# The softmax of a pair of heads, in operations common to both heads

## What is computed

```python
for i in range(S // Q_BLOCK):                 # two blocks of 128 queries
    s0, e = i * Q_BLOCK, (i + 1) * Q_BLOCK
    sc = (jnp.einsum('bqhd,bkhd->bhqk', q_nope[:, s0:e], k_nope[:, :e])
          + jnp.einsum('bqhr,bkr->bhqk', q_pe[:, s0:e], k_pe[:, :e]))
    sc = sc.astype(jnp.float32) * ATTN_SCALE
    mask = jnp.arange(e)[None, :] <= (s0 + jnp.arange(Q_BLOCK))[:, None]
    sc = jnp.where(mask, sc, -jnp.inf)
    p = jax.nn.softmax(sc, axis=-1).astype(v.dtype)
    outs.append(jnp.einsum('bhqk,bkhd->bqhd', p, v[:, :e]))
```

## Time and profile before

| | us |
|---|---|
| median of 3 runs | 1775.51 |
| lowest, highest | 1775.25, 1775.96 |
| the profiled execution | 1775.12 |
| its span, first to last instruction | 1773.2 |
| PE busy | 1762.1 (99%) |
| DVE busy | 1133.2 (64%) |
| ACT busy | 914.8 (52%) |
| POOL busy | 112.7 (6%) |

### The profile page before, as it was taken

One profiled execution on the slowest core, in us unless ns is written; L12 is line 12 of the kernel. 1 busy time (PEld: TensorE's weight loads), 2 busy tenths in 40 slices (PEclk: granted clock), 3 DMA queues, 4 the chain that ended last, 5 costly groups with the idle time before them and its releaser, 6 DMA issues.

```text
span 1773.2 us, 29180 instructions
## 1 busy us (share of the span) xinstructions
PE 1762.1 (99%) x10370; PEld 1560.7 (88%) x10370; DVE 1133.2 (64%) x1456; ACT 914.8 (52%) x1174; POOL 112.7 (6%) x132
## 2 busy tenths in 40 slices
PE   9999999999999999999999999999999999999998
PEld 5888888888888888889999888888888888888886
DVE  5766666556666666678997776666655566666553
ACT  6666664334444453456775456666533344445433
POOL 2200000000000001123111420000000000000000
PEclk9999999999999999999999999999999999999999
DMA  7555557545555566544445555555655455556642
GB/s 274 198 189 189 189 193 233 185 160 178 189 188 189 189 223 196 175 154 147 158 136 167 190 189 189 189 189 189 226 201 167 165 189 189 189 189 222 227 144 72
DMA packets 85728, 328.78 MB, mean 185 GB/s; under 512 B 9648, under 2 KB 10800, under 8 KB 85552
## 3 DMA queue, kind: packets, MB, share of 16 engines
q1 hardware_dynamic: 85536, 327.09, 55.1%
q10 hardware_dynamic: 144, 1.05, 0.2%
HBM read 326.01 MB, written 2.10 MB: 185 GB/s over the span
## 4 chain that ended last, share of the span: by engine, by line
PE 97%; DVE 2%; ACT 1%; issue 0%; POOL 0%; ACTq 0%; DVEq 0%; POOLq 0%
PE ps L427 57%; PE ps L428 31%; PE ps L497 1%; PE ps L435 1%; PE ps L437 1%; PE ps L436 1%; PE ps L787 1%; PE ps L786 1%; PE ps L788 1%; DVE w_lo L1210 0%; PE ps L623 0%; PE ps L625 0%; PE ps L624 0%; DVE xg L1220 0%; PE ps L677 0%; DVE x L1272 0%
## 5 line engine op out<-in xcount | busy, mean ns | idle before, releaser
L1210 DVE TENSOR_TENSOR w_lo<-raw,w_hi 128x1024 fp32r<-128x1024 f32 (+2 forms) x564 | 736.7, 1309 | 420.6 <-ACT w_hi L831 418.7
L427 PE MATMUL ps<-xg,w_hi 128*128 128x512 f32 x2880 | 999.7, 390 | 0.2 <-DVE w_lo L1210 0.2
L831 ACT ACTIVATE w_hi<-raw 128x1024 fp32r<-128x1024 f32 (+2 forms) x565 | 631.9, 1120 | 552.9 <-PE ps L428 537.1
L428 PE MATMUL ps<-xg,w_lo 128*128 128x256 f32 x2880 | 812.1, 282 | 0.0
L427 PEld LDWEIGHTS ps<-xg,w_hi 128*128 128x128 f32 x2880 | 540.7, 188 | 113.8 <-DVE w_lo L1210 0.6
L428 PEld LDWEIGHTS ps<-xg,w_lo 128*128 128x128 f32 x2880 | 544.3, 189 | 0.1
L427 PE MATMUL ps<-act,w_hi 128*128 128x512 f32 x1320 | 458.0, 390 | 0.0
L428 PE MATMUL ps<-act,w_lo 128*128 128x256 f32 x1320 | 372.2, 282 | 0.0
L427 PEld LDWEIGHTS ps<-act,w_hi 128*128 128x128 f32 x1320 | 247.8, 188 | 51.9
L428 PEld LDWEIGHTS ps<-act,w_lo 128*128 128x128 f32 x1320 | 249.5, 189 | 0.0
L1290 DVE TENSOR_TENSOR sums<-ps,cross 128x512 f32<-128x512 f32 x88 | 60.9, 692 | 95.5 <-ACT cross L908 95.2
(11 more groups left out here) (196 smaller groups left out, 1217.4 us busy)
## 6 DMA issues: line engine op xcount, KB each, us to landing
raw<-w_gate SPq DMA_DIRECT2D x176, 512.0 KB, 3.2
raw<-w_up SPq DMA_DIRECT2D x176, 512.0 KB, 3.2
raw<-w_down SPq DMA_DIRECT2D x120, 704.0 KB, 4.2
raw<-w_o SPq DMA_DIRECT2D x32, 512.0 KB, 3.2
raw<-w_last SPq DMA_DIRECT2D x11, 512.0 KB, 3.2
raw<-w_q_a SPq DMA_DIRECT2D x8, 512.0 KB, 3.2
raw<-w_kv_a SPq DMA_DIRECT2D x8, 512.0 KB, 3.2
raw<-w_q_nope SPq DMA_DIRECT2D x8, 512.0 KB, 3.7
```

Source lines behind the costliest of these rows:

```text
L427: pe.matmul(ps[:, bank, :], w_hi[:, s, j * P:(j + 1) * P], moving, start=start, stop=False)
L428: return pe.matmul(ps[:, bank, 0:SEQ], w_lo[:, s, j * P:(j + 1) * P], moving[:, 0:SEQ], start=False, stop=stop)
L831: nc.scalar.activation(dst, src, ACT.Copy).then_inc(hi_ready, 1)
L1210: nc.vector.tensor_tensor(lo, src, hi.bitcast(F32), ALU.subtract).then_inc(lo_ready, 1)
```

## The change

`row_max` and `normalise` now treat both heads of a pair in one call. `row_max` waits until the scores of both heads are there. The mask addition of the first block is one instruction for both heads, with the mask read twice through a broadcast. The two reductions of the second block follow, then one negation for both heads, then the cosine product (`rope_cos`, which stood between the heads), the two reductions of the first block and one negation. ACT waits once for the second block of both heads and does their two exponentials, then once for the first block of both and does theirs. `normalise` waits for all four, takes one reciprocal of four values a partition in place of two of two values each, and scales in four instructions as before. The targets of the waits change with the count; a pass of the loop has 12 counted steps on DVE in place of 16.

```diff
-            def exps(g, hh, i):
-
-                sc.wait_ge(max_ready, plus(4 * g + 2 * hh + 1, i, 8))
-                nc.scalar.activation(prob[:, hh, P:], prob[:, hh, P:], ACT.Exp, bias=stat[:, hh, 3:4],
-                                     accum_out=stat[:, hh, 5:6]).then_inc(exp_ready, 1)
-                sc.wait_ge(max_ready, plus(4 * g + 2 * hh + 2, i, 8))
-                nc.scalar.activation(prob[:, hh, 0:P], prob[:, hh, 0:P], ACT.Exp, bias=stat[:, hh, 2:3],
-                                     accum_out=stat[:, hh, 4:5]).then_inc(exp_ready, 1)
+            def exps(g, i):
+
+                sc.wait_ge(max_ready, plus(2 * g + 1, i, 4))
+                for hh in range(2):
+                    nc.scalar.activation(prob[:, hh, P:], prob[:, hh, P:], ACT.Exp, bias=stat[:, hh, 3:4],
+                                         accum_out=stat[:, hh, 5:6]).then_inc(exp_ready, 1)
+                sc.wait_ge(max_ready, plus(2 * g + 2, i, 4))
...
@@ -1486,28 +1486,35 @@
                                         heads[:, plus(g, i, 2), :, 0:SEQ].bitcast(F32),
                                         ALU.subtract).then_inc(head_split, 1)
 
-            def row_max(g, hh, i):
-
-                ve.wait_ge(scores_ready, plus(2 * g + hh + 1, i, 4))
-
-                scored, first, second = ps[:, SCORES + hh, :], prob[:, hh, 0:P], prob[:, hh, P:]
-                begun(nc.vector.tensor_tensor(first, scored[:, 3 * P:], const[:, C_MASK + P:C_MASK + 2 * P], ALU.add))
-                begun(nc.vector.tensor_tensor_reduce(second, scored[:, P:3 * P], const[:, C_MASK:C_MASK + 2 * P],
-                                                     ATTN_SCALE, -3.0e38, ALU.add, ALU.max, stat[:, hh, 1:2]))
+            def row_max(g, i, beside=lambda: None):
+
+                ve.wait_ge(scores_ready, plus(2 * g + 2, i, 4))
+                scored, both = ps[:, SCORES:SCORES + 2, :], prob[:, :, 0:P]
+                mask = const[:, C_MASK + P:C_MASK + 2 * P].rearrange("p (o t) -> p o t", o=1).broadcast_to([P, 2, P])
+                begun(nc.vector.tensor_tensor(both, scored[:, :, 3 * P:], mask, ALU.add))
+                for hh in range(2):
+                    begun(nc.vector.tensor_tensor_reduce(
+                        prob[:, hh, P:], scored[:, hh, P:3 * P], const[:, C_MASK:C_MASK + 2 * P], ATTN_SCALE, -3.0e38,
+                        ALU.add, ALU.max, stat[:, hh, 1:2]))
                 settled()
-                nc.vector.tensor_scalar(stat[:, hh, 3:4], stat[:, hh, 1:2], -1.0, None, ALU.mult).then_inc(max_ready, 1)
-                step(nc.vector.tensor_tensor_reduce(first, scored[:, 0:P], first, ATTN_SCALE, -3.0e38, ALU.add,
-                                                    ALU.max, stat[:, hh, 0:1]))
-                nc.vector.tensor_scalar(stat[:, hh, 2:3], stat[:, hh, 0:1], -1.0, None, ALU.mult).then_inc(max_ready, 1)
-
-            def normalise(g, hh, i):
-
-                ve.wait_ge(exp_ready, plus(4 * g + 2 * hh + 2, i, 8))
-                step(nc.vector.reciprocal(stat[:, hh, 6:8], stat[:, hh, 4:6]))
-                nc.vector.tensor_scalar(prob[:, hh, 0:P], prob[:, hh, 0:P], stat[:, hh, 6:7], None,
-                                        ALU.mult).then_inc(prob_ready, 1)
-                nc.vector.tensor_scalar(prob[:, hh, P:], prob[:, hh, P:], stat[:, hh, 7:8], None,
-                                        ALU.mult).then_inc(prob_ready, 1)
+                nc.vector.tensor_scalar(stat[:, :, 3:4], stat[:, :, 1:2], -1.0, None, ALU.mult).then_inc(max_ready, 1)
+                beside()
+                for hh in range(2):
+                    begun(nc.vector.tensor_tensor_reduce(
+                        prob[:, hh, 0:P], scored[:, hh, 0:P], prob[:, hh, 0:P], ATTN_SCALE, -3.0e38, ALU.add, ALU.max,
+                        stat[:, hh, 0:1]))
+                settled()
+                nc.vector.tensor_scalar(stat[:, :, 2:3], stat[:, :, 0:1], -1.0, None, ALU.mult).then_inc(max_ready, 1)
+
+            def normalise(g, i):
+
+                ve.wait_ge(exp_ready, plus(4 * g + 4, i, 8))
+                step(nc.vector.reciprocal(stat[:, :, 6:8], stat[:, :, 4:6]))
+                for hh in range(2):
+                    nc.vector.tensor_scalar(prob[:, hh, 0:P], prob[:, hh, 0:P], stat[:, hh, 6:7], None,
+                                            ALU.mult).then_inc(prob_ready, 1)
+                    nc.vector.tensor_scalar(prob[:, hh, P:], prob[:, hh, P:], stat[:, hh, 7:8], None,
+                                            ALU.mult).then_inc(prob_ready, 1)
 
             lat_norm(KV, 1, G_LKV, beside=(key_scale, lambda: None))
 
...
@@ -1526,11 +1533,8 @@
                 else:
                     if g >= 2:
                         heads_lo_half(g - 2, i)
-                    row_max(g - 1, 0, i)
-                    rope_cos(g, i)
-                    row_max(g - 1, 1, i)
-                    normalise(g - 1, 0, i)
-                    normalise(g - 1, 1, i)
+                    row_max(g - 1, i, beside=lambda: rope_cos(g, i))
+                    normalise(g - 1, i)
                     pair_lo(g, 1, q_buf, i)
                     split(n + SPLIT_SLOTS, i)
                     split(n + 1 + SPLIT_SLOTS, i)
@@ -1543,7 +1547,7 @@
 
             slot(0)
             slot(1)
-            loop(HG // 2 - 2, 2 * 8, lambda i: (slot(2, i), slot(3, i)))
+            loop(HG // 2 - 2, 2 * 6, lambda i: (slot(2, i), slot(3, i)))
             slot(HG - 2)
             slot(HG - 1)
 
```

More of the change, by code:

```diff
@@ L1051, in heads_hi_half @@
                                      ACT.Copy).then_inc(head_hi, 1)
-            def exps(g, hh, i):
-                sc.wait_ge(max_ready, plus(4 * g + 2 * hh + 1, i, 8))
-                nc.scalar.activation(prob[:, hh, P:], prob[:, hh, P:], ACT.Exp, bias=stat[:, hh, 3:4],
-                                     accum_out=stat[:, hh, 5:6]).then_inc(exp_ready, 1)
-                sc.wait_ge(max_ready, plus(4 * g + 2 * hh + 2, i, 8))
-                nc.scalar.activation(prob[:, hh, 0:P], prob[:, hh, 0:P], ACT.Exp, bias=stat[:, hh, 2:3],
-                                     accum_out=stat[:, hh, 4:5]).then_inc(exp_ready, 1)
+            def exps(g, i):
[5 more added lines that the diff above has]
+                for hh in range(2):
+                    nc.scalar.activation(prob[:, hh, 0:P], prob[:, hh, 0:P], ACT.Exp, bias=stat[:, hh, 2:3],
+                                         accum_out=stat[:, hh, 4:5]).then_inc(exp_ready, 1)
             def slot(g, i=None):
@@ L1082, in slot @@
                     split(n + SPLIT_SLOTS, i)
-                    exps(g - 1, 0, i)
-                    exps(g - 1, 1, i)
+                    exps(g - 1, i)
                     pair_hi(g, 1, q_buf, i)
@@ L1111, in _ @@
             split(n1 + SPLIT_SLOTS)
-            exps(HG - 1, 0, None)
-            exps(HG - 1, 1, None)
+            exps(HG - 1, None)
             split(n1 + 1 + SPLIT_SLOTS)
@@ L1553, in _ @@
             split(n1 + SPLIT_SLOTS)
[L1554 to L1557, removed]
+            row_max(HG - 1, None)
+            normalise(HG - 1, None)
             split(n1 + 1 + SPLIT_SLOTS)
```

## The result

The changed kernel takes 1780.64 us (median of 8 runs, 1780.15 to 1781.23) against 1775.30 for the kernel before (8 runs): 1.0031 of its time, 95% interval 1.0022 to 1.0041. It is slower, by 5.3 us where 5.1 was forecast (1780.6). One execution of neg_single, a kernel among the experiments, took 2171.76 us at a granted clock of 0.752 of full speed and is left out of its median.

A forecast was written before the change was run, and what follows sets the result against it. PE was taken as the bound, stalled by late L1480. Slots 2 to 6 cost 3.35 us, slot 1 0.37, slot 7 1.01, total 4.73; with 0.35 for issue, +5.1 on 1775.51 gives 1780.6 us, range 1777.0 to 1783.2.

The forecast's parts named there:

- (a): DVE's wait for both heads' scores: first mask moves by 0.94 us, to 0.32 behind the last score product's start.
- (b): From first mask addition to reciprocal, through reductions, negations and ACT's four exponentials: reciprocal starts 3.37 us after the mask.
- the open read: Accumulator's read behind the first of two reductions, shown by no row: taken as 0.05 us, bounds 0 and 0.12.
- (c): Normalisation, up to L1453: one reciprocal of 0.20 us and four scalings of 0.94 together, none overlapping POOL.
- (d): Instruction savings already counted; in the output projection's slot, later scaling put at nothing, or 0.6 us without cover.
- the issue gaps: Idle time at the cosine product in slot 2, now before the second negation: 0.35 us for both loop passes.
- the bounds that were given: Path from the first mask, for reads, semaphores and POOL: -0.16 to +0.36 us in each of seven slots.
- The first rival: Not slower: DVE's shorter work decides, not ACT's chain; mask to L1453 under 3.91 us, 1774.7 us; chance 0.12.
- The second: Rival: PE's stall comes but is under half, starts 0.3 us earlier; 2.6 us lost, 1778.1; chance 0.16.
- third: Rival: more is lost, issue gaps in both loop passes and POOL's collision in each slot; 6.9 us, 1782.4 up; chance 0.12.

The follow-up runs named there:

- neg_single: The changed kernel with each common negation of two elements a partition made by two instructions of one element; 1779.97 us, ratio 1.0026 to the kernel before.
- wait_both: The kernel before, except that the row maxima of either head wait for the scores of both heads; 1778.18 us, ratio 1.0016.
- both_waits: The kernel before with both waits of the change (both heads' scores, all four exponentials) and none of its common operations; 1782.31 us, ratio 1.0040.

## Why the prediction was right

(a) The wait for both scores. The mask was put at T0 + 0.32; it is there in the changed kernel, in wait_both and in both_waits.

(b) Mask to reciprocal, put at 3.37, is 3.52 (873.05 to 876.57). First negation at 1.14, put at 1.19: the first reduction's read and the second reduction start together, at 873.73, so the open read cost 0, the lower bound. Second negation at 2.18, put at 2.19. The step that was mis-sized stands behind it: the third exponential was put at 2.40 and is at 2.61, 0.21 late, because of the negation's 0.40 us beside POOL; 0.17 of it are gone where neg_single negates by heads. The prediction asked of the scalings whether POOL is at work, and not of the negation. The trace of before couldn't warn of it by a row, for its negations had one element, and lasted 0.15 even within POOL's instruction (872.87). The Trainium skill could, "VectorE: DVE Perf Modes", on what auto-detection actually checks: a single-source operation with its source and destination in SBUF, whose outermost dimension that isn't 1 is even in both, takes the mode of both ports. Two heads make two elements. The runs agree, with 0.40 against 0.15 beside POOL. The exponentials were put at 0.51, 0.51, 0.39 and 0.48 and fit (0.51, 0.49, 0.40 and 0.48); the semaphore to the reciprocal took 0.03 (876.54 to 876.57), not 0.10, and gave 0.07 back.

(c) Reciprocal to L1453: put at 1.14, measured 1.14 (876.57 to 877.71). No scaling ran beside POOL.

(d) The last slot was put at nothing. T0 to L696 is 9.21 there in both kernels.

Slot by slot, the growth of the distance from one T0 to the next, forecast and measured: slot 1 0.37 and 0.47, slot 2 0.67 and 0.94, slot 3 0.67 and 0.80, slot 4 0.67 and 0.91, slots 5 and 6 0.67 each and 0.83 and 0.75, slot 7 1.01 and 1.09. The forecast's sum with its 0.35 for the issue gaps is 5.1, the stage's is 5.79 in this execution, which was the longest of the eight, and the medians differ by 5.3. The excess of 0.08 to 0.16 in slots 1, 3, 5, 6 and 7 is the negation less the small savings. Of the issue gaps 0.1 remained in slot 2 and 0.1 in slot 4, 0.2 for 0.35. The path from the mask to L1453 is thus 0.15 longer than forecast (4.66 for 4.51), inside the bounds that were given. That 1780.6 stands so close to 1780.64 is luck: the difference was put 0.2 too low by the medians and 0.7 too low by the stage, and it was added to a median of 1775.51, 0.2 above that of the eight runs.

The first rival, in which the shorter instruction list decides, is excluded: DVE does 5 us less and the kernel is 5 us slower, and mask to L1453 is 4.66, not under 3.91. The second and third were sizes of the same mechanism. The second's 2.6 us lie below the interval (3.9 to 7.3 us); the third's 6.9 lie within it, and only the stage's 5.79 speaks against them. The third's collision exists, but at another instruction and with 0.2 us a slot.

## What to carry to other kernels

A merge of two chains that ran as a pipeline (maxima, exponentials, scaling of one head under those of the other) turns two short waits into two long ones; count the instructions saved only after the idle time that each engine gains between its steps. Before that, look for the one consumer that pays, and its slack in microseconds: here 0.4 us, after which everything was paid in full and two delays that were cheap alone were dear together. And the cheapest cure was neither version: the work that stands in line ahead of the late operation, but isn't needed for long, went behind it. That move takes 6.2 us from the changed kernel; what it gives the kernel before, 0.5 us by the medians, isn't told from nothing.

## What the runs showed of the hardware

A tensor_scalar of two elements a partition, source and destination in SBUF, that starts 0.37 to 0.38 us behind the start of a POOL tensor_tensor lasts 0.39 to 0.40 us and ends 0.02 to 0.03 behind POOL's end; without POOL it lasts 0.17. One of one element lasts 0.14 to 0.16 in both cases, and a reciprocal of two elements 0.17 beside POOL. Two reductions with an accumulator's read, with no wait between them, follow each other without any gap for the read (both start at 873.73 in the changed kernel); with a wait the next instruction starts 0.12 us behind the read (874.07 and 874.19).
